# MLP products alternated on the way down, a modulation load behind two weight loads, a block of weight sums first

## What is computed

```python
def sq_relu_mlp(h, w1, w2):
    return jnp.square(jax.nn.relu(h @ w1)) @ w2          # 512x1024 @ 1024x4096, then @ 4096x1024

def ada_params(cond, w_ada, b_ada):
    m = jax.nn.silu(cond) @ w_ada + b_ada                # 1024 @ 1024x6144, one per layer and condition
```

## Time and profile before

| | |
|---|---|
| median of 3 runs | 2388.97 us (2382.45 to 2391.66) |
| the profiled execution | 2389.52 us, of which the span of the profile 2387.7 us |
| TensorE busy (matmuls) | 2233.5 us, 94% of the span |
| VectorE / ScalarE / GpSimd busy | 1033.9 / 395.7 / 66.5 us |
| mean granted TensorE clock | 0.977 of full speed |
| the MLP stage | 286.9 to 695 us of the span |
| TensorE's waits of over 1 us in 280 to 700 us | 8.0 us for the first activations, 2.7 us at the stage's end, 2.4 us in unit 6, 1.1 us in unit 4 and 1.2 us in unit 10 |

### The profile page before, as it was taken

How to read it: one execution, slowest core, us unless ns; L and a number is a source line. 1 busy time by engine, 2 the same in 40 slices (tenths; PEclk the granted TensorE clock), 3 DMA queues, 4 the chain that set the end, 5 groups by cost and what they waited for, 6 DMA issues and landing times.

```text
span 2387.7 us, 24615 instructions
## 1 busy us (share of the span) xinstructions
PE 2233.5 (94%) x9962; PEld 1287.3 (54%) x9962; DVE 1033.9 (43%) x1408; ACT 395.7 (17%) x743; POOL 66.5 (3%) x74
## 2 busy tenths in 40 slices
PE   7999899999999999779799999996999799999998
PEld 3343488888874456555444444443886444444443
DVE  3883488787736630881312222215443312222223
ACT  3224221012024210660200000002000200000000
POOL 1000100000010000001000000001000000000000
PEclk9999999999999999999799999998999799999999
DMA  9216135677511112000699999998200589999996
GB/s 357 115 47 239 71 141 179 245 267 259 214 62 35 36 36 75 32 1 1 248 429 428 428 428 428 428 429 329 81 1 1 211 366 420 430 428 428 429 428 268
DMA packets 105800, 565.76 MB, mean 237 GB/s; under 512 B 8440, under 2 KB 17150, under 8 KB 78078
## 3 DMA queue, kind: packets, MB, share of 16 engines
q1 hardware_dynamic: 105296, 564.60, 58.5%
q10 hardware_dynamic: 430, 0.13, 0.0%
HBM read 562.61 MB, written 2.10 MB: 237 GB/s over the span
## 4 chain that ended last, share of the span: by engine, by line
PE 64%; issue 22%; DMA 6%; DVE 5%; ACT 1%; POOL 0%; SPq 0%; DVEq 0%; ACTq 0%; POOLq 0%
PE psum L1291 21%; PE psum L1079 14%; PE psum L1632 10%; DMA ring<-in_moe_w_gate_dram 4%; PE psum L1448 3%; PE psum L1647 3%; PE psum L1691 2%; PE psum L1559 2%; PE psum L1241 1%; PE psum L1523 1%; DVE small L2157 1%; PE psum L1099 1%; DMA ring<-in_moe_w_down_dram 1%; PE psum L1496 1%; DMA ring<-in_ada_w_dram 1%
## 5 line engine op out<-in xcount | busy, mean ns | idle before, releaser
L1632 PE MATMUL psum<-ring,arena 128*64 128x512 f32 x3072 | 671.4, 595 | 28.4 <-DMA ring<-in_moe_w_gate_dram 20.4
L1632 PEld LDWEIGHTS psum<-ring,arena 128*64 128x64 f32 x3072 | 228.4, 137 | 457.0 <-issue 454.9
L1079 PE MATMUL psum<-hT,ring 128*128 128x512 f32 x608 | 267.5, 598 | 3.0 <-ACT hT L712 3.0
L2297 DVE SCALAR_TENSOR_TENSOR xT<-psum,modv,xT 128x512 f32<-128x512 f32 x128 | 96.1, 751 | 235.1 <-PE psum L1691 223.1
L1079 PEld LDWEIGHTS psum<-hT,ring 128*128 128x128 f32 x608 | 116.0, 192 | 148.6 <-issue 141.4
L1291 PE MATMUL psum<-hT,ring 128*128 128x256 f32 x608 | 141.8, 391 | 15.8 <-ACT hT L712 15.8
L1291 PE MATMUL psum<-ring 128*128 128x256 f32 x640 | 144.5, 383 | 2.4 <-DVE rstd L2019 2.4
L1291 PEld LDWEIGHTS psum<-hT,ring 128*128 128x128 f32 x608 | 119.2, 197 | 36.1 <-issue 19.0
L1291 PEld LDWEIGHTS psum<-ring 128*128 128x128 f32 x640 | 122.4, 192 | 22.0 <-issue 5.3
L1647 PEld LDWEIGHTS psum<-arena 128*128 128x128 f32 x1024 | 120.7, 197 | 15.5 <-issue 15.5
L1647 PE MATMUL psum<-arena 128*128 128x128 f32 x1024 | 124.9, 282 | 3.9 <-DVE arena L2307 3.9
(11 more groups left out here) (283 smaller groups left out, 2335.2 us busy)
## 6 DMA issues: line engine op xcount, KB each, us to landing
ring<-in_moe_w_gate_dram SPq DMA_DIRECT2D x64, 2048.0 KB, 15.6
ring<-in_moe_w_up_dram SPq DMA_DIRECT2D x64, 2048.0 KB, 17.2
ring<-in_moe_w_down_dram SPq DMA_DIRECT2D x64, 2048.0 KB, 17.2
ring<-in_ada_w_dram SPq DMA_DIRECT2D x24, 2048.0 KB, 8.0
ring<-in_mlp_w_dram SPq DMA_DIRECT2D x16, 2048.0 KB, 8.2
ring<-in_w_mod_dram SPq DMA_DIRECT2D x12, 2048.0 KB, 12.6
ring<-in_conv_w_in_dram SPq DMA_DIRECT2D x6, 2048.0 KB, 18.8
ring<-in_attn_w_in_dram SPq DMA_DIRECT2D x5, 2048.0 KB, 8.0
```

What stands on the lines that cost most here:

```text
L1079: ins = pe.matmul(bank[:, 0:width], w[:, k, col:col + P], src(k), start=start and k == 0, stop=stop and k == kts - 1)
L1632: ins = pe.matmul(psum[64 * e:64 * e + 64, bank + nh, :], src[:, 4 * h + k, 64 * e:64 * e + 64], w[:, k, nh * N:(nh + 1) * N], start=h == ...
L2297: dve.scalar_tensor_tensor(out=xT[:, fj, :], in0=psum[:, SCATTER[fj % 3], :], scalar=modv[:, 1 + 2 * layer, 40 + fj:41 + fj], in1=xT[:, fj ...
```

## The change

It has five edits.

- In `w2_unit` the products of steps A and B alternate: A0, B0, A1, B1 instead of A0, A1, B0, B1. `begin` of bank t+3 moves to the top. The semaphore `mlp_part` is counted up in another order, so that B0 is now its first count and A1 its second.
- `m1_copy` on ScalarE waits for that second count, and the modulation row due there is moved first (`at + 3`).
- `w_sums_4` of a unit's first block waits for the first count instead of the second.
- In `MLP_LOADS` mod 11 goes behind w8 and w9.
- In unit 6 VectorE makes the sums s1, s3 and s2 of w9 first, and then the five modulation steps that stood ahead of them.

```diff
-             ("mod", 11), ("w", 8), ("w", 9), ("mod", 12), ("mod", 13), ("mod", 14), ("w", 10), ("mod", 15), ("mod", 16),
+             ("w", 8), ("w", 9), ("mod", 11), ("mod", 12), ("mod", 13), ("mod", 14), ("w", 10), ("mod", 15), ("mod", 16),
...
                     at = 56 * half + 28 + 14 * nh
-                    mods_before(at + 2)
-                    m1_copy(6 * half + 4 + nh, T_W2[half] + 4 * nh, 22 * half + 12 + 5 * nh + 1)
+                    mods_before(at + 3)
+                    m1_copy(6 * half + 4 + nh, T_W2[half] + 4 * nh, 22 * half + 12 + 5 * nh + 2)
...
                 begin(t + 1)
+                begin(t + 3)
                 for kq in range(2):
                     arrived(pe, B_W[bs[kq]])
                     pe.wait_ge(S["hid_ready"], 16 * half + 4 + 8 * kq)
                     ins = product(t + 1, w_quarter(slots[kq], 0, 0), hid_quarter(kq, 0, 0), kq == 0)
                     if kq:
                         ins.then_inc(S["mlp_part"], 1)
-                    after(at + kq)
-                begin(t + 3)
-                for kq in range(2):
+                    after(at + 2 * kq)
                     pe.wait_ge(S["mlp_tsum"], ts + 1 + 2 * kq)
                     pe.wait_ge(S["mlp_wsum"], 3 * bs[kq] + 1)
                     product(t + 3, sums[kq][0], t1[kq], kq == 0).then_inc(S["mlp_part"], 1)
-                    after(at + 2 + kq)
+                    after(at + 1 + 2 * kq)
...
-                else:
+                elif unit != 6:
                     mod_steps(5)
                 w_sums_13(b + 1)
                 if not last:
                     dve.wait_ge(S["mlp_part"], 22 * half + 3 * v + 2)
                     w_sums_2(b + 1)
+                if unit == 6:
+                    mod_steps(5)
                 mod_steps(n - 13)
...
-                dve.wait_ge(S["mlp_part"], part + 2)
+                dve.wait_ge(S["mlp_part"], part + 1)
                 w_sums_4(b)
```

## The result

| | before | after |
|---|---|---|
| median | 2383.77 us (2382.26 to 2391.66, 10 runs) | 2394.84 us (2392.39 to 2401.58, 10 runs) |
| ratio | | 1.0045, 95% interval 1.0035 to 1.0055 |
| span of the profile | 2387.7 us | 2395.5 us |

The change makes the kernel 10.7 us slower (0.0045 of 2384). The forecast was +9.9 us, 2399.2 us in a range of 2392 to 2405: the measured median lies in the range, and the sign is right. The median is 4.4 us under the forecast time, and the median of the kernel before came out 5.2 us lower with ten runs than with the three that I had, so the level that I started from accounts for all of that distance. The interval is 0.1% to either side, so a loss of this size is clear of the noise; I had taken 0.5% for the limit.

The account below looks back on a forecast made before the run. TensorE, busy 94% of the span, was taken to bound the kernel. Unit 6's 11.0 us late, plus 0.3 in unit 7, minus 1.44 in unit 10, gave +9.9 us: 2399.2 us, range 2392 to 2405.

Parts of the forecast that it names:

- step 120 can run: VectorE's first step that reads mod 11: forecast to run at 497.8, against 481.04 in the kernel before.
- VectorE's wait: VectorE, at step 120 by about 480, stands still some 18 us until the moved mod 11 lands.
- product B of unit 6: TensorE's product B waits for s1 of w8 and starts at 504.7, a stall of 13.2 us.
- F: TensorE's product F in unit 6, decided by VectorE: starts at 523.1, 12.8 us later, and takes 3.5 us instead of 5.22.
- w10 later relative to TensorE: Unit 7: w10 follows mod 14 more closely in the queue and lands an estimated 1.4 us later; slack leaves 0.3 us.
- units 4 and 10: Alternated products remove product A1's waits for w5 and w13: gains of 1.36 us in unit 4, 1.44 us in unit 10.
- The clock's cost after the long stall: TensorE's slow clock after the stall at product B of unit 6: 2.8 us, mostly hidden while VectorE decides F.
- The gain of the three other edits: MLP stage without the moved load: alternation 1.36 and 1.44 us, w9 sums first 4.31 us, in all 7.1 us.
- the 4.31 us for the sums of w9: Unit 6, sums moved ahead of the modulation steps: F's stall (2.54 us) and its slow product (1.77 us) vanish.
- Rival A: Mod 11's lateness at step 120 is absorbed, only the gains remain: 2382.4 us; chance 0.09.
- Rival B: Short waits at F of units 6 and 7 lower the clock too: +12 to +14, 2403 us; chance 0.19.
- Rival C: Mod 11 lands before w9, shortening VectorE's chain by 6.2 us: +3.7, 2393.2 us; chance 0.04.

Follow-up runs that it names:

- e2: The kernel before with only mod 11's load moved behind w8 and w9: ratio to before 1.0049, stage +12.5 us.
- e5: The changed kernel with mod 11 issued between w8 and w9: ratio to before 1.0023, stage +4.0 us.
- e4: The kernel before with only the sums of w9 put ahead of the five modulation steps in unit 6: ratio 0.9990, stage -2.5 us.
- e7: e6 with w10 issued ahead of mod 14 and the sums of w10 ahead of unit 7's modulation steps: ratio to before 0.9994, stage -2.9 us.
- e1: The changed kernel with mod 11's load put back ahead of w8 and w9, other edits kept: ratio to before 0.9973, stage -6.0 us.
- e8: e1 with steps 124 to 127 put between s3 and s2 of w9 in unit 6: ratio to before 0.9968, stage -6.4 us.
- e6: The changed kernel with mod 11's first four steps (120 to 123) moved from unit 5 to behind the sums of w9 in unit 6: ratio to before 1.0016, stage +1.4 us.

## Why the prediction was right

The mechanism and its size came out, step by step (unit 4 begins 0.16 us later in the profile after than in the one before, so its times are that much late):

| step | forecast | profile after |
|---|---|---|
| step 120 can run | 497.8 | 497.64 |
| VectorE's wait | some 18 us | 17.73 us |
| product B of unit 6 | 504.7 | 504.54 |
| F | 523.1 | 522.85 |
| G | 526.6 | 526.38 |
| w10 later relative to TensorE | 1.4 us | from unit 7's A to the first sum of w10 5.80 us before, 7.18 us after: 1.4 us |
| unit 7's F | 0.3 us | E to F 547.75 - 544.09 - 3.45 = 0.2 us |
| units 4 and 10 | no wait | no wait |
| the stage | +9.9 us | +9.5 us |

- What gave this precision: the third place in the line of DMAs was in the old trace, taken by another block, and VectorE's queue behind the late step keeps its offsets while it is the engine waited for.
- The 1.4 us for w10 was picked between two ends and not worked out from a row. That it came out to the tenth is luck; at most 0.3 us of the sum hung on it.
- The clock's cost after the long stall was mis-sized, 2.8 us in the forecast, 12.13 - 10.52 = 1.6 us in the profile. TensorE therefore came to F earlier and waited 1.53 us instead of 0.6. VectorE decided F, as forecast, and the sum did not move. In e2 the cost was 2.7 us after 12.5 us, in e5 2.6 us after 7.2 us. So the cost did not grow with the length of the wait. The first product after the stage's first wait of 7.95 us, up to which all the kernels run the same instructions, took 6.36 to 6.68 us in ten of the twelve profiles and 5.19 and 5.33 us in two (e4, e7), against 3.62 us at full clock. The Trainium skill (TensorE: Matmul & The Clock Gate, what's actually happening) says that the number of slow matmuls at a kernel's start differs from run to run of one kernel; I had read it for any start out of idling. This spread agrees, though the two low values are from other kernels than the rest; the two kernels that were profiled twice gave 6.41 and 6.36 us, and 6.38 and 6.37 us.
- The gain of the three other edits was given as 7.1 us; it is 6.0 us (e1). The term that failed is the 4.31 us for the sums of w9: they brought 3.2 us there. 0.7 us of the rest is at F of unit 6: I had not counted that s2 waits for product B once it stands first. The other 0.4 us is at F of unit 7: the later w10, which I had counted for the changed kernel, comes in e1 to e5 and in e8 too (7.22 to 7.61 us), and I had put it at nothing there. In the changed kernel s2 did not matter, since VectorE came there after B.
- Rival A fell: nothing absorbed the late load. Rival B fell: the wait of 1.53 us did not lower the clock, F took 3.53 us, and unit 7 cost 0.2 us. Rival C fell: mod 11 landed after w9 in the changed kernel, 5.4 us behind it, and in e5 ahead of it only because it was issued ahead of it. The rule of the Trainium skill on issuing early (DMA: Bandwidth & Descriptors, rules for kernel authors) held here: 15.5 us lie between e1 and the changed kernel, whose only difference is the place of that load. Waiting late alone, with the load still late, gave back 8.1 of them (e6).

Not tried: w10 ahead of mod 14 with its sums left where they stood. Why the clock fell after 2.4 us in one kernel and not in the other stays open.

## What to carry to other kernels

Where one queue issues all loads in order, each behind a wait for its slot, moving a load means moving it behind the waits of those ahead; take their issue times from the trace, and look for the first instruction that reads it. What counts is what stands behind that reader on its engine: 17.7 us of a helper engine's standing still became 12.7 us on the engine that bounds, and none of it was in the work that the late block served. Gains of separate edits need not add up: where two of them remove the same lateness, it is gained once.

## What I had not expected of the hardware

The same idle time of TensorE, 2.38, 2.37, 2.38 and 2.26 us, was followed by a stretch at 1.2 GHz in both profiles of one kernel (F took 5.2 us) and by 2.4 GHz throughout in both profiles of another (3.5 us). The clock was still at full speed in the wait, and fell about half a microsecond after TensorE had begun to work again. A wait of 4.72 us in e6 was followed by 0.68 over the product, waits of 1.77, 1.79 and 2.18 us by products of full speed (3.69 us).
